# Splitting fp32 weight tiles in a hybrid decoder layer: the high part cast by ScalarE, the low part subtracted by VectorE

## The reference, cut to what matters

```python
n = rms_norm(h, ln_mix_pre[l])
(da_q, da_k, da_v, dn_q, dn_k, dn_v, dn_z, dn_b, dn_a, ca_q, gate_logits) = [
    n @ wp for wp in jnp.split(w_in[l], SPLIT_IDX, axis=-1)]
...
proj = jnp.einsum('bsiw,iwd->bsid', ys, w_branch[l])
gates = jax.nn.sigmoid(gate_logits.reshape(B, S, N_BRANCH, D_MODEL))
mixed = jnp.sum(gates * proj, axis=2)
h = h + rms_norm(mixed @ w_out[l], ln_mix_post[l])

n = rms_norm(h, ln_ff_pre[l])
f = jnp.square(jax.nn.relu(n @ w_ff1[l])) @ w_ff2[l]
h = h + rms_norm(f, ln_ff_post[l])
```

## Time and profile before

| | before |
|---|---|
| time, median of 3 runs | 1530.51 us (1529.88 to 1531.38) |
| span of the profiled execution | 1529.8 us |
| PE busy | 1438.2 us (94%) |
| DVE busy | 794.4 us (52%) |
| POOL busy | 732.8 us (48%) |
| ACT busy | 291.5 us (19%) |
| mean granted PE clock | 0.978 |
| DMA | 142.78 MB, mean 93 GB/s |

### The profile page before, as it was taken

How to read it: one execution, slowest core, us unless ns; L and a number is a source line. 1 busy time by engine, 2 the same in 40 slices (tenths; PEclk the granted TensorE clock), 3 DMA queues, 4 the chain that set the end, 5 groups by cost and what they waited for, 6 DMA issues and landing times. The chain is left out here.

```text
span 1529.8 us, 18731 instructions
## 1 busy us (share of the span) xinstructions
PE 1438.2 (94%) x7540; PEld 1204.2 (79%) x7540; DVE 794.4 (52%) x1243; ACT 291.5 (19%) x562; POOL 732.8 (48%) x380
## 2 busy tenths in 40 slices
PE   5868999989999899999899989999979999999998
PEld 5668878868888788888678878787778888888887
DVE  6885237543377776854764223577455541144312
ACT  4112222222223232232132210000122100011100
POOL 4347733236531335422356454766555764466551
PEclk9989999999999999999999999999998999999998
DMA  5134222112202212101312242754521323223221
GB/s 192 56 124 152 76 69 69 55 70 79 82 26 90 76 37 81 63 28 66 107 41 77 97 144 97 239 182 150 178 70 42 99 94 97 96 97 97 91 89 55
DMA packets 46413, 142.78 MB, mean 93 GB/s; under 512 B 4944, under 2 KB 7416, under 8 KB 46328
## 3 DMA queue, kind: packets, MB, share of 16 engines
q1 hardware_dynamic: 46328, 141.59, 28.0%
HBM read 126.88 MB, written 16.27 MB: 94 GB/s over the span
## 5 line engine op out<-in xcount | busy, mean ns | idle before, releaser
L723 POOL TENSOR_TENSOR w_lo<-w_raw,w_hi 128x1024 fp32r<-128x1024 f32 x200 | 486.5, 2433 | 651.0 <-DVE w_hi L1118 651.0
L1515 PE MATMUL acc<-n_hi,w_hi 128*128 128x512 f32 (+1 forms) x984 | 400.3, 407 | 3.8 <-DVE n_lo L1403 2.4
L1118 DVE CAST w_hi<-w_raw 128x1024 fp32r<-128x1024 f32 x200 | 160.9, 807 | 441.7 <-PE acc L1517 253.8
L1517 PE MATMUL acc<-n_hi,w_lo 128*128 128x512 f32 (+1 forms) x984 | 384.5, 391 | 0.0
L1516 PE MATMUL acc<-n_lo,w_hi 128*128 128x512 f32 (+1 forms) x984 | 384.2, 390 | 0.0
L1515 PEld LDWEIGHTS acc<-n_hi,w_hi 128*128 128x128 f32 x984 | 189.3, 192 | 42.4 <-issue 3.7
L1517 PEld LDWEIGHTS acc<-n_hi,w_lo 128*128 128x128 f32 x984 | 188.3, 191 | 40.9
L1516 PEld LDWEIGHTS acc<-n_lo,w_hi 128*128 128x128 f32 x984 | 189.3, 192 | 35.3 <-issue 1.0
L1517 PE MATMUL acc<-h_hi,w_lo 128*128 128x512 f32 x256 | 101.0, 395 | 0.0
L1515 PE MATMUL acc<-h_hi,w_hi 128*128 128x512 f32 x256 | 101.0, 395 | 0.0
L1516 PE MATMUL acc<-h_lo,w_hi 128*128 128x512 f32 x256 | 101.0, 395 | 0.0
(11 more groups left out here) (311 smaller groups left out, 2172.8 us busy)
## 6 DMA issues: line engine op xcount, KB each, us to landing
w_raw<-weights SPq DMA_DIRECT2D x200, 512.0 KB, 3.5
gate_scratch<-gate_st SPq DMA_DIRECT2D x24, 256.0 KB, 2.1
g_in<-gate_scratch SPq DMA_DIRECT2D x24, 256.0 KB, 3.8
y_raw<-y_scratch SPq DMA_DIRECT2D x16, 256.0 KB, 3.5
x_tok<-x SPq DMA_DIRECT2D x4, 512.0 KB, 5.0
y_scratch<-y_st SPq DMA_DIRECT2D x4, 512.0 KB, 3.3
y_scratch<-d_ET SPq DMA_DIRECT2D x4, 512.0 KB, 3.5
y_scratch<-y_st SPq DMA_DIRECT2D x8, 256.0 KB, 2.6
```

The costliest lines, as they stand in the source:

```text
L723: nc.gpsimd.tensor_tensor(w_lo[:, t % SPL], w_raw[:, t % RAW], w_hi[:, t % SPL].bitcast(F32), ALU.subtract).then_inc(lo_ready, 1)
L1118: V_.tensor_copy(w_hi[:, t % SPL], w_raw[:, t % RAW]).then_inc(hi_ready, 1)
L1515: mm(bank, wh, hi_of(k), start=start and k == 0, stop=False)
L1517: last = mm(bank, wl, hi_of(k), start=False, stop=stop and k == KT - 1)
```

## The change

Who makes the two halves of a weight tile changes, and where in each queue it stands. The cast to `w_hi` leaves DVE for ACT. The subtraction to `w_lo` leaves POOL for DVE, as an instruction with two inputs in SBUF. The loads (SP) and the matmuls (PE) are untouched, and so are the waits that guard the buffers.

```diff
 @block.gpsimd
-            def split_lo(t):
-                if t < NT:
-                    pool.wait_ge(hi_ready, t + 1)
-                    if t >= SPL:
-                        pool.wait_ge(tile_used, t - SPL + 1)
-                    nc.gpsimd.tensor_tensor(w_lo[:, t % SPL], w_raw[:, t % RAW],
-                                            w_hi[:, t % SPL].bitcast(F32), ALU.subtract).then_inc(lo_ready, 1)
...
             for slot, (main, ev, fi, sa, sd) in enumerate(SLOTS):
-                if ev is not None:
-                    split_lo(ev + SPL)
-                    if TILES[ev][0] == "gate":
-                        n = n_gate[ev]
-                        pool.wait_ge(acc_free, ev + 1)
-                        nc.gpsimd.tensor_scalar(gate_st[:], gate_st[:], 0.5, 0.5, ALU.mult,
-                                                ALU.add).then_inc(gs_ready, 1)
+                if ev is not None and TILES[ev][0] == "gate":
+                    pool.wait_ge(acc_free, ev + 1)
+                    nc.gpsimd.tensor_scalar(gate_st[:], gate_st[:], 0.5, 0.5, ALU.mult, ALU.add).then_inc(gs_ready, 1)
...
 @block.scalar
+            def split_hi(t):
+
+                if t < NT:
+                    act.wait_ge(ld[t % RAW], 16 * (t // RAW + 1))
+                    if t >= SPL:
+                        act.wait_ge(tile_used, t - SPL + 1)
+                    nc.scalar.copy(w_hi[:, t % SPL], w_raw[:, t % RAW]).then_inc(hi_ready, 1)
...
                 if ev is not None:
                     evacuate(ev)
+                    split_hi(ev + SPL)
...
+            def between():
+
+                for e in range(KT - H, KT + 1):
+                    out_part(e)
+                split_hi(T_F1)
+                for e in range(KT + 1, len(OUT_PARTS) - 1):
+                    out_part(e)
+                square_row(0)
+                split_hi(T_F1 + 1)
+                out_part(len(OUT_PARTS) - 1)
+                square_row(1)
+                split_hi(T_F1 + 2)
...
 @block.vector
-            def split_hi(t):
+            def split_lo(t):
                 if t < NT:
-                    dve.wait_ge(ld[t % RAW], 16 * (t // RAW + 1))
-                    if t >= SPL:
-                        dve.wait_ge(tile_used, t - SPL + 1)
-                        dve.wait_ge(lo_ready, t - SPL + 1)
-                    V_.tensor_copy(w_hi[:, t % SPL], w_raw[:, t % RAW]).then_inc(hi_ready, 1)
+                    dve.wait_ge(hi_ready, t + 1)
+                    V_.tensor_tensor(w_lo[:, t % SPL], w_raw[:, t % RAW], w_hi[:, t % SPL].bitcast(F32),
+                                     ALU.subtract).then_inc(lo_ready, 1)
...
-                if ev is not None:
-                    split_hi(ev + SPL)
                 if sd is not None:
                     delta(sd)
                 if sa is not None:
                     attn(sa)
+                if ev is not None:
+                    split_lo(ev + SPL)
                 if ev in n_conv:
                     conv(ev)
```

More of the change, by code:

```diff
@@ L729, in _ @@
             for j in POOL_ROWS:
-                if j <= ST:
-                    split_lo(j // 2)
                 pool.wait_ge(su_hi, j + 1)
@@ L823, in _ @@
                     gain_row(1)
-                for j in range(k):
-                    split_lo(t0 + j + SPL)
                 if r < N_BR and r // KT == 2:
@@ L870, in _ @@
                 nc.scalar.mul(x_tok[:, j], x_tok[:, j], sml[:, 8 + j:9 + j]).then_inc(su_norm2, 1)
+            split_hi(0)
             for j in range(ST):
                 row_hi(j)
+                if j in (1, 3):
+                    split_hi((j + 1) // 2)
             for j in range(ST, N_SU):
@@ L1054, in row_hi2, with square_hidden @@
                 nc.scalar.copy(n2_hi[:, :, i * P:(i + 1) * P], blocks(two(back(i)))).then_inc(n2h, 1)
-            for e in range(len(OUT_PARTS) - 1):
-                out_part(e)
-            square_row(0)
-            out_part(len(OUT_PARTS) - 1)
-            square_row(1)
-            for i in range(2):
-                scale_row(i)
-            for i in range(2):
-                row_hi2(i)
-            for i in range(2, ST):
-                square_row(i)
-            for i in range(2, ST):
-                scale_row(i)
-            for i in range(2, ST):
-                row_hi2(i)
-            for f in range(DFF // P):
+            T_F1 = LATE[L_F1[0]][1]
+            def between():
[9 more added lines that the diff above has]
+                split_hi(T_F1 + 2)
+                for i in range(2):
+                    scale_row(i)
+                for i in range(2):
+                    row_hi2(i)
+                for i in range(2, ST):
+                    square_row(i)
+                for i in range(2, ST):
+                    scale_row(i)
+                for i in range(2, ST):
+                    row_hi2(i)
+            def square_hidden(f):
                 act.wait_ge(relu_ok, f + 1)
@@ L1076, in _, with square_f @@
                 nc.scalar.activation(sq[:, f % 2], relu[:, f % 2], ACT.Square).then_inc(sq_ok, 1)
-            for m in range(KT):
+            def square_f(m):
                 act.wait_ge(f_ev, KT + m + 1)
@@ L1084, in _ @@
                 nc.scalar.mul(f_T[:, m], f_T[:, m], par[:, PC_POST + KT + m:PC_POST + KT + m + 1]).then_inc(fg_ok, 1)
+            for r, (tile, t0, k) in enumerate(LATE):
+                if tile[0] == "out":
+                    if tile[1] < KT - H:
+                        out_part(tile[1])
+                    elif tile[1] == KT - H:
+                        between()
+                elif tile[0] == "f1":
+                    square_hidden(tile[1])
+                if not (tile[0] == "out" and tile[1] >= KT - H):
+                    for j in range(k):
+                        split_hi(t0 + j + SPL)
+                if r >= L_F2[1]:
+                    square_f(tile[1] % KT)
         @block.vector
@@ L1148, in _ @@
             dve.wait_ge(in_par, 16)
-            split_hi(0)
             gain(0)
             gain(1)
-            split_hi(1)
+            split_lo(0)
             gain(2)
@@ L1155, in _ @@
             gain(3)
+            split_lo(1)
             row_lo(3)
-            split_hi(2)
+            split_lo(2)
             rms_of_two(ST)
@@ L1408, in _ @@
                     y_hi_tile(r - 1)
-                for j in range(k):
-                    split_hi(t0 + j + SPL)
                 bank = result_bank(r)
@@ L1424, in _ @@
                             V_.tensor_copy(mx_hi[:, m], mix_acc[:, m]).then_inc(mxh_ready, 1)
+                    split_lo(t0 + SPL)
+                elif tile[0] == "out" and tile[1] < KT - H:
+                    split_lo(t0 + SPL)
                 elif r == N_BR + KT - H:
+                    split_lo(t0 + SPL)
                     rms_of_f(1, 0, 2, ps_d[:, 2])
@@ L1430, in _ @@
                         norm_row(0, i)
+                    split_lo(t0 + SPL + 1)
                 elif r == N_BR + KT - 1:
@@ L1456, in _ @@
                         V_.tensor_tensor(f_T[:, m], f_T[:, m], bank, ALU.add).then_inc(f_ev, 1)
+                    for j in range(k):
+                        split_lo(t0 + j + SPL)
             rms_of_f(3, 0, ST, ps_d[:, 2])
```

## The result

The changed kernel takes 1497.4 us (median of 4 runs, 1493.82 to 1500.34), the kernel before 1530.95 (4 runs); the ratio is 0.9776, 95% interval 0.9761 to 0.9792. The forecast was 1498. The profiled execution has a span of 1496.0 us and its own time is 1497.8: 1.8 us lie outside the span.

The account below looks back on a forecast made before the run. PE was taken to wait at single places for chains over DVE and ACT. Savings of 6.5 + 9 + 9.5 + 1.6 + 6.2 = 32.8 us from 1529.8 gave 1497.0, plus 0.7 to the median: 1498 us, range 1480 to 1517.

Parts of the forecast that it names:

- 12 to 121 us, -6.5: First stage: shorter tanh chains and two conflicts gone, less 1.0 us at the start; 6.5 us saved, bounds +3 and -16.
- the 3.3 and 4.2: First stage: 3.3 us from 0.65 less on each of five tiles' tanh chains, 4.2 from two single conflicts.
- even: First stage, memory tiles: about 1.2 us longer wait behind dk's subtraction, offset by one conflict less in dk.
- 121 to 900 us, -9: Middle: a third of 26.6 us of gaps, mostly at DVE's or ACT's chains, goes; 9 us saved, between -20 and +8.
- The first rival: Nearly all conflicts were on the path: 18 us saved in the middle, 5 more of early clock; 1483 us, chance 0.17.
- 900 to 970 us, -9.5: POOL finishes the gate at once, so DVE's row comes some 7 us earlier; 9.5 us saved with clock, between -12 and -3.
- 970 to 1092 us, -1.6: Two gaps behind DVE's 2.40 us adds go; 1.6 of 1.7 us saved.
- 1092 to 1165 us, -6.2: ACT's row scaling waits less for small DVE instructions that met POOL; 6.2 us saved including clock, between -10 and 0.
- Span to median, 0.7: Whole kernel: the median time was taken to lie 0.7 us above the profiled span.
- DVE and POOL blocking each other further: DVE's 200 subtractions meet POOL's remaining 246 us, at most 39 us of DVE time; 1515 us, chance 0.22.
- POOL as cover: POOL's subtraction costs nothing and PE's waits are the chains' own length; 1530 us, chance 0.05.
- ACT in line: ACT's casts wait for loads ahead of copies PE needs, 69 us at worst; 1565 us, slower, chance 0.06.

Follow-up runs that it names:

- e4: Kernel before, with POOL's subtraction issued as two instructions of 128x512 instead of one of 128x1024: 1531.0 us, ratio 0.9996.
- e7: Kernel after, with POOL also making one subtraction of 128x1024 that nobody reads in each of 51 middle slots: 1522.7 us.
- e8: Kernel after, with POOL also making two memsets of 128x1024 on a tile nobody reads in each of 51 middle slots: 1500.2 us.
- e9: Kernel after, with DVE subtracting only one of eight blocks of the low part in 51 middle slots, the rest left out: 1489.5 us.
- e3: Kernel before, with only the subtraction moved from POOL to DVE; the cast stays on DVE, one cast placed differently: 1506.4 us.
- e1: Kernel before, with POOL finishing a gate tile ahead of its subtraction in the same slot: 1519.5 us, ratio 0.9915.
- e2: Kernel before, with only the cast moved from DVE to ACT; the subtraction stays on POOL: 1551.5 us, ratio 1.0126.

## Why the prediction was right, step by step

**The sum was right, at 1498 for 1497.4, and the gate's queue with it; in the first and the middle stage terms of the wrong size came out near the right sum, which is luck.**

- *The bound.* That PE waits at single places for chains over DVE and ACT, and that a last stage without idle time gives nothing, held.
- *Conflicts.* That DVE stands still until POOL's instruction is over: e4 and e7 show it, e8 shows for which operands. POOL also stands still beside DVE, which the prediction left out of POOL's sum: its subtractions for `mx_lo` take 2206 ns after and 1287 before, and it is busy 259 us and not 246.
- *DVE, ACT, POOL busy.* Forecast 770, 500, 246; measured 773, 483, 259. The subtraction on DVE takes 1453 ns and not 1226, because it meets what POOL still has: 200 x 0.227 = 45 us, close to the 39 at most that the rival had worked out. DVE "shrinks by the conflicts" by 152 us, where 770 supposed 794 + 84 - 770 = 108. So 773 against 770 is luck: two terms were some 45 us too small, with opposite signs.
- *12 to 121 us, -6.5; measured -8.7.* The chain from tanh to tanh was forecast at 6.1 us and is 6.11. Two terms were mis-sized. The start costs 3.5 us (end of tile 0 at 28.6 before, 32.1 after) and not 1.0: the first main matmul starts 1.0 us later, as forecast (20.8 for 19.8), and the other 2.5 are clock. PE had stood still for 4.3 us ahead of it (before 1.5), and these windows, of before and of after, show the granted clock behind:

```profile
19.80:28.60 8.80, 8.80 (x72) 8.59 (x72) 7.62 (x6) 3.25 (x5) 6.89 (x3) 1.00 0.20 61
...
20.80:26.20 5.40, 5.38 (x25) 5.40 (x26) 5.40 (x4) 4.20 (x6) 2.15 (x1) 0.50 0.21 57
```

The granted clock is 0.50 there, the lower of its two levels (1.2 for 2.4 GHz), and the wait ahead of it was the longer one. And the rest of the stage gave 12.2 and not the 3.3 and 4.2. The memory tiles were "even": 5.7 us in two gaps before, one gap of 5.4 after.
- *121 to 900 us, -9; measured -7.1.* The size held; a third of the gaps was a guess, with no term for DVE's own subtractions behind the steps, which cost some 8 us in 51 slots (e9). What the conflicts cost depends on the trigger: 25 us for the 51 that e7 puts back with ACT's cast ahead of them, and by the estimate under e9 about 10 us for all that stood in the middle before. With 25 and 8 the middle should have given about 17, and it gave 7.1, so these two do not make up the term, and no run takes POOL's subtraction away without giving it to DVE. Moving the subtraction alone left the stage from tile 26 to 98 as it was (699.2 against 697.4, in the slowest of e3's four executions); with the cast it is 693.8. The first rival's 18 us for the middle did not come.
- *900 to 970 us, -9.5; measured -10.9,* and e1 by itself 11.0 there. Step, place and queue as forecast.
- *970 to 1092 us, -1.6; measured -2.6.* The adds are free.
- *1092 to 1165 us, -6.2; measured -5.6,* and the remaining conflict with `rows` was forecast.
- *1165 to 1514 us, 0.* No idle time before or after; the 1.4 us more come and go with the same code.
- *Span to median, 0.7; measured 1.8.* The span of before was set against a median of other runs; an execution's own time lies 1.7 to 1.9 us above its span (up to 2.1 in e7). The sum would have been 1499.
- *The rivals.* DVE and POOL blocking each other further costs those 45 us of DVE time, not my 17 us of the kernel's; the advice of the Trainium skill, page "Perfetto Trace Analysis", section "Optimizing Scalar/DVE Operations", that offloading between GpSimd and DVE might not help, did not hold here: e3 moves only that, and takes 25 us off, 13 of them beyond what the gate's place in POOL's queue is worth (e1). POOL as cover is refuted. ACT in line is refuted for the change (16.7 us of waits for loads in ACT's casts), and e2, a kernel that none of my rivals was about (the cast on ACT with the subtraction left on POOL), is slower for a reason that stays open.

## What to carry to other kernels

Where a DVE instruction takes as long as a POOL instruction beside it, compare it with its twin elsewhere in the trace: the difference is standing still. What a microsecond of it costs is read by stages: nothing where PE never waits, 0.65 us in e7, about 0.2 in the middle before. Cutting POOL's work in pieces does not help if what it saves lies where PE never waits. Before moving work off an engine, look for the short step that stands behind the long one in its queue: a swap of two rows gave a third of this gain. And cost the two halves of a change apart as well as together: here one half alone is a loss, of which the other makes a gain.

## What the runs showed of the hardware

- A POOL memset, which reads nothing, still held up DVE's `tensor_scalar` of 128x512 (1.13 us for 0.48) in the same trace in which multiply-adds beside it kept their length.
- The blocked time counts in DVE's busy time: the page showed DVE at 52% before and after, 168 us of it standing still before and 16 after. Busy shares alone could not have told these two kernels apart.
- The same matmuls (1512 or 1513 begin there) of the last stage, without a gap and at a granted clock of 1.00, lasted 345.9 us in some executions and 347.3 in others, 0.4% apart.
